# A six-stage layer stack on one core: head pairs' running sums on separate rows, second tile turned first, reordered seams

## What is computed

```python
x = layer_norm(ALPHA * x + ffn, ln_ffn_g, ln_ffn_b)        # end of stages 1 and 3
# stage 4, scan
a_cs = cumsum(dt * A)                                       # per head, over 256 tokens
m = (C @ B.T) * exp(a_cs[l] - a_cs[s])  (s <= l)            # 16 heads
y = m @ (x * dt) + d_skip * x
y = rms_norm((y * silu(z)).reshape(.., 4 groups, 256))      # squares summed by group
# stages 4 and 5, attention group of 8 heads
q, k = rope(rms_norm(q)), rope(rms_norm(k))
o = softmax(mask(q @ k.T / 8)) @ v
```

## Time and profile before

| | us |
|---|---|
| median of 3 runs | 1745.08 (1743.03 to 1753.56) |
| profiled execution, its own time | 1750.59 |
| its span, first to last instruction | 1748.8 |
| TensorE busy | 1618.3 (93%) |
| VectorE, ScalarE, GpSimd busy | 369.8, 269.0, 85.1 |
| mean granted clock of TensorE | 0.988 |

### The profile page before, as it was taken

How to read it: one execution, slowest core, us unless ns; L and a number is a source line. 1 busy time by engine, 2 the same in 40 slices (tenths; PEclk the granted TensorE clock), 3 DMA queues, 4 the chain that set the end, 5 groups by cost and what they waited for, 6 DMA issues and landing times.

```text
span 1748.8 us, 24093 instructions
## 1 busy us (share of the span) xinstructions
PE 1618.3 (93%) x10356; PEld 993.2 (57%) x10356; DVE 369.8 (21%) x796; ACT 269.0 (15%) x647; POOL 85.1 (5%) x148
## 2 busy tenths in 40 slices
PE   8998999988988899989999899888999999999988
PEld 7855555555554576465555555545884444645553
DVE  0933000000000212430000000003324442330322
ACT  2011000000000012210000000001232323311330
POOL 0000000000000000000000000000001233003110
PEclk9999999999999899999999999999999999999998
DMA  9557999999999832579999999998442223244100
GB/s 399 217 217 316 426 428 428 428 426 430 427 427 427 367 144 97 217 315 426 427 428 428 428 428 428 428 427 375 145 145 96 96 97 108 85 144 144 49 0 24
DMA packets 37632, 502.55 MB, mean 287 GB/s; under 512 B 4160, under 2 KB 4288, under 8 KB 5440
## 3 DMA queue, kind: packets, MB, share of 16 engines
q1 hardware_dynamic: 36992, 499.53, 69.3%
q0 software_dynamic: 576, 2.10, 0.3%
HBM read 500.56 MB, written 1.05 MB: 287 GB/s over the span
## 4 chain that ended last, share of the span: by engine, by line
PE 75%; DMA 18%; DVE 3%; issue 2%; ACT 1%; SPq 0%; ACTq 0%; DVEq 0%
DMA ring<-in_expert_up 14%; PE ps L1116 12%; PE ps L614 10%; PE ps L737 9%; PE ps L754 8%; PE ps L802 6%; PE ps L651 6%; PE ps L720 3%; DMA ring<-in_expert_down 3%; PE ps L820 3%; PE ps L1111 2%; PE ps L966 2%; PE ps L942 2%; PE ps L1170 1%; PE ps L591 1%
## 5 line engine op out<-in xcount | busy, mean ns | idle before, releaser
L737 PE MATMUL ps<-x_tok,constants_sb 128*128 128x256 f32 x1184 | 296.8, 394 | 0.0
L754 PE MATMUL ps<-ring,arena 128*32 128x256 f32 x3968 | 240.2, 384 | 44.4 <-DMA ring<-in_expert_up 37.9
L737 PEld LDWEIGHTS ps<-x_tok,constants_sb 128*128 128x128 f32 x1184 | 213.8, 191 | 103.0 <-issue 80.4
L1116 PE MATMUL ps<-ring,spare 128*128 128x512 f32 x480 | 215.5, 603 | 1.8 <-DVE spare L1799 1.7
L754 PEld LDWEIGHTS ps<-ring,arena 128*32 128x32 f32 x3968 | 120.7, 110 | 153.1 <-DMA ring<-in_expert_up 32.0
L614 PE MATMUL ps<-spare,ring 128*128 128x256 f32 x832 | 183.0, 383 | 4.0 <-DVE spare L1799 1.7
L614 PEld LDWEIGHTS ps<-spare,ring 128*128 128x128 f32 x832 | 159.4, 192 | 26.4 <-DVE spare L1796 2.9
L1116 PEld LDWEIGHTS ps<-ring,spare 128*128 128x128 f32 x480 | 89.5, 191 | 111.1 <-issue 108.5
L802 PE MATMUL ps<-ring,arena 128*32 128x512 f32 x960 | 123.2, 613 | 16.0 <-ACT arena L1462 12.0
L2002 DVE TENSOR_TENSOR arena<-arena,ps 128x128 f32<-128x128 f32 x64 | 18.4, 288 | 507.3 <-ACT arena L1467 507.3
L651 PE MATMUL ps<-ring,arena 128*128 128x512 f32 x224 | 101.3, 610 | 1.9 <-DVE arena L2430 1.4
(11 more groups left out here) (279 smaller groups left out, 1291.5 us busy)
## 6 DMA issues: line engine op xcount, KB each, us to landing
ring<-in_expert_up SPq DMA_DIRECT2D x124, 2048.0 KB, 22.7
ring<-in_expert_down SPq DMA_DIRECT2D x46, 2048.0 KB, 26.6
ring<-in_stream SPq DMA_DIRECT2D x44, 2048.0 KB, 8.6
ring<-in_expert_down SPq DMA_DIRECT2D x28, 1024.0 KB, 24.8
arena<-in_expert_up SPq DMA_DIRECT2D x4, 2048.0 KB, 8.2
arena<-in_expert_down SPq DMA_DIRECT2D x2, 2048.0 KB, 10.6
spare<-in_expert_down SPq DMA_DIRECT2D x2, 2048.0 KB, 7.6
constants_sb<-in_constants SPq DMA_DIRECT2D x1, 1574.0 KB, 17.2
```

Source lines behind the costliest of these rows:

```text
L737: pe.matmul(ps[:, b, 0:TOK], ident, x[:, 0, 0:TOK], start=True, stop=True, skip_group_check=True)
L754: ins = pe.matmul(ps[q * SLOTS:(q + 1) * SLOTS, 4 + e % 2, 0:TOK] .rearrange("p (g n) -> p g n", g=2), xg[:, 4 * half + k, e * SLOTS:(e + ...
L1116: ins = pe.matmul(bank(b + part), xT[:, k, part * P:(part + 1) * P], w[:, k, :], start=(k == 0), stop=(k == KT - 1))
```

## The change

1. Bias rows of the norm behind an expert stage: right behind the scatter, ahead of the branch (before: behind it). If the branch is taken they are made again.
2. Warm-ups: in the last quad five instead of four behind each up chunk, four instead of two between down projections; none instead of five at the head of stage 2; nine instead of thirteen at the head of stage 4.
3. The 16 running sums are also put on partitions 64 to 79; `run_sum` of an odd head reads them there.
4. In the scan's last round y(7) and the last projection half stand ahead of the last two square sums.
5. Attention: in the first group of a stage the wait for the last projection's take-up moves behind the first scores, and the wait for `ss_var` behind the first tile's transposes. In the other groups the second tile is turned first, and the wait stands between the tiles; `move_T` on ScalarE and VectorE follows that order.

```diff
@@ -583,7 +583,7 @@
 
-                for b in range(2 * tiles[0], 2 * tiles[-1] + 2):
+                for b in [2 * t + kk for t in tiles for kk in range(2)]:
                     t, kk = b // 2, b % 2
@@ -761,7 +761,7 @@
                             if not (closing and j == 2 * QUAD - 1):
-                                spin(6)
+                                spin(6, SPINS + 1 if closing else SPINS)
                             if opening and j == 0:
@@ -807,10 +807,10 @@
                             pe.wait_ge(s("back_moved"), i + (n2 + 1))
-                            closing()
+                            closing(0)
                         elif closing and k < 3:
                             pe.wait_ge(sem("ln_gain_moved"), rnd + 1)
-                            spin(4, SPINS // 2)
+                            spin(4)
                         elif k < 3 and not closing:
@@ -821,6 +821,8 @@
                         ins.then_inc(s("scattered"), 1)
+                    if closing:
+                        closing(1)
 
@@ -905,7 +907,7 @@
                           lambda j: slot4[slot(b0 + QUAD_CHUNKS + j)],
-                          lambda: norm_rows(0).then_inc(sem("ln_rows"), 1))
+                          lambda which: norm_rows(which).then_inc(sem("ln_rows"), 1))
                 pe.wait_ge(sem("m_counted"), layer + 1)
@@ -920,13 +922,10 @@
                                       None, lambda j: slot4[j % RING])
-                    pe.sem_inc(sem(f"m{layer}_more_over"), 1)
-                norm_rows(1).then_inc(sem("ln_rows"), 1)
+                    norm_rows(1).then_inc(sem(f"m{layer}_more_over"), 1)
 
...
                 g = base[STICK]
-                if MOE0 in on:
-                    keep_warm(5)
                 transposes("x2", x, normed(STICK), (0,))
@@ -1131,12 +1130,19 @@
 
-            def attention(grp, ahead, extra=None):
+            def attention(grp, ahead, extra=None, opening=False):
+                taken_up = projected[0]
+                def ready(t, kk):
+                    if opening and SSD in on and grp == 0 and (t, kk) == (1, 0):
+                        pe.wait_ge(sem("ss_var"), 1)
+                    elif not opening and (t, kk) == (0, 0):
+                        pe.wait_ge(sem("at_proj"), taken_up)
 
                 pe.wait_ge(sem("at_qk"), 2 * (grp + 1))
-                pe.wait_ge(sem("at_proj"), projected[0])
-                transposes(qk_turn(grp), at_qk)
+                transposes(qk_turn(grp), at_qk, ready, (0, 1) if opening else (1, 0))
                 wait_T(qk_turn(grp))
@@ -1196,6 +1202,8 @@
                         mix(pr - 1)
+                    elif opening:
+                        pe.wait_ge(sem("at_proj"), taken_up)
                     turn_p(pr)
@@ -1207,7 +1215,7 @@
                 if MOE1 in on:
-                    keep_warm(13)
+                    keep_warm(9)
                 transposes("h4", at_h, ready, (0,))
@@ -1229,10 +1237,13 @@
                 sums = con[:, CONST["upto"][0]:CONST["ones"][1]]
-                pe.matmul(ps[0:16, 1, 64:64 + TOK], av[:, 0, :], sums, start=True, stop=False,
-                          skip_group_check=True)
-                pe.matmul(ps[0:16, 1, 64 + P:64 + TOK], av[:, 1, :], C("upto"), start=False,
-                          stop=True, skip_group_check=True).then_inc(sem("ss_cs"), 1)
+                for p0 in (0, 64):
+                    pe.matmul(ps[p0:p0 + 16, 1, 64:64 + TOK], av[:, 0, :], sums, start=True,
+                              stop=False, skip_group_check=True)
+                for p0 in (0, 64):
+                    ins = pe.matmul(ps[p0:p0 + 16, 1, 64 + P:64 + TOK], av[:, 1, :], C("upto"),
+                                    start=False, stop=True, skip_group_check=True)
+                ins.then_inc(sem("ss_cs"), 1)
 
@@ -1262,7 +1273,7 @@
                               start=True, stop=True).then_inc(sem("ss_bc"), 1)
-                pe.wait_ge(sem("ss_csT"), 1)
+                pe.wait_ge(sem("ss_csT"), 2)
                 pe.wait_ge(sem("ss_z"), 2)
@@ -1271,8 +1282,11 @@
                         pe.wait_ge(sem("ss_cb"), h + 1)
-                    pe.matmul(ps[:, 4 + h % 2, 0:TOK], ident[0:16, h:h + 1].broadcast_to([16, P]),
-                              ss_csT[0:16, :], start=True, stop=True).then_inc(sem("ss_sum"), 1)
+                    p0 = 64 * (h % 2)
+                    pe.matmul(ps[:, 4 + h % 2, 0:TOK],
+                              ident[p0:p0 + 16, p0 + h:p0 + h + 1].broadcast_to([16, P]),
+                              ss_csT[p0:p0 + 16, :], start=True, stop=True)\
+                        .then_inc(sem("ss_sum"), 1)
 
@@ -1306,15 +1320,15 @@
                         half(*units.pop(0))
-                    if n >= 2:
+                    if 2 <= n < SSD_HEADS // 2:
                         square_sums(n - 2)
...
                         half(*units.pop(0))
+                square_sums(SSD_HEADS // 2 - 2)
                 square_sums(SSD_HEADS // 2 - 1)
-                pe.wait_ge(sem("ss_var"), 1)
-                attention(0, [(kind, g + 9 + n) for n, kind in enumerate("qkv")])
+                attention(0, [(kind, g + 9 + n) for n, kind in enumerate("qkv")], opening=True)
                 attention(1, [(kind, g + 12 + n) for n, kind in enumerate("qkv")])
@@ -1349,7 +1363,8 @@
                 no = 1 if SSD in on else 0
-                attention(g_no(3), [(kind, g + 4 + n) for n, kind in enumerate("qkv")])
+                attention(g_no(3), [(kind, g + 4 + n) for n, kind in enumerate("qkv")],
+                          opening=True)
 
@@ -1389,10 +1404,10 @@
 
-            def move_T(name, dst, scale=1.0, banks=None):
-                for b in banks or ((0, 2) if name[0] == "q" else (0, 1)):
-                    act.wait_ge(transposed, 4 * turn[name] + b + 1)
+            def move_T(name, dst, scale=1.0, banks=None, order=range(4)):
+                for b in banks or (0, 1):
+                    act.wait_ge(transposed, 4 * turn[name] + order.index(b) + 1)
                     kk = b % 2
@@ -1599,7 +1614,10 @@
             def attention(grp, out_g, ahead, between=lambda pr: None):
-                move_T(qk_turn(grp), at_qkT, 0.125)
+                if grp in (0, g_no(3)):
+                    move_T(qk_turn(grp), at_qkT, 0.125, (0, 2))
+                else:
+                    move_T(qk_turn(grp), at_qkT, 0.125, (2, 0), (2, 3, 0, 1))
 
@@ -1783,13 +1801,11 @@
 
-            def move_T(name, dst, banks=None, column=None):
-                if banks is None:
-                    banks = (1, 3) if name[0] == "q" else (2, 3)
+            def move_T(name, dst, banks=(2, 3), column=None, order=range(4)):
...
                     kk = b % 2
-                    dve.wait_ge(transposed, 4 * turn[name] + b + 1)
+                    dve.wait_ge(transposed, 4 * turn[name] + order.index(b) + 1)
                     o = dst[:, 4 * kk:4 * kk + 4, (b // 2) * P:(b // 2 + 1) * P]
@@ -2090,6 +2106,7 @@
                                 .then_inc(sem(f"m{layer}_more_lowered"), 1)
+                    dve.wait_ge(sem(f"m{layer}_more_over"), 1)
                 if stage == MOE1 and SSD in on:
@@ -2180,7 +2197,10 @@
                           last=lambda: None):
-                move_T(qk_turn(grp), at_qkT)
+                if grp in (0, g_no(3)):
+                    move_T(qk_turn(grp), at_qkT, (1, 3))
+                else:
+                    move_T(qk_turn(grp), at_qkT, (3, 1), order=(2, 3, 0, 1))
 
@@ -2277,8 +2297,9 @@
                     d[7], ps[:, 1, 0:32].rearrange("p (t h) -> p t h", t=2), -1.0, None, mul))
-                dve.tensor_copy(ss_csT[0:16, :], ps[0:16, 1, 64:64 + TOK])\
-                    .then_inc(sem("ss_csT"), 1)
+                for p0 in (0, 64):
+                    dve.tensor_copy(ss_csT[p0:p0 + 16, :], ps[p0:p0 + 16, 1, 64:64 + TOK])\
+                        .then_inc(sem("ss_csT"), 1)
                 hd = [P, 8, 64]
```

## The result

The changed kernel takes **1732.83 us** (median of 4 runs, 1731.70 to 1734.14) and the kernel before, beside it on the same chip, 1745.09 (4 runs, 1743.03 to 1753.56). The ratio is 0.9917 with the interval 0.9896 to 0.9937: faster by 0.8%, less than the 1% from which the forecast speaks of faster. The forecast was 1732. The profiled execution took 1732.98 (span 1730.8), 17.6 less than that of before. That is more than the 13.4 forecast, and the two profiles also differ in where and for how long the clock was low: read in stretches of 1 us, some 42 us of before and 34 us of the changed kernel were at 1.2 GHz. So the places are compared by their own lengths, and even these hold some of the clock, as the experiments show.

The account below looks back on a forecast made before the run. The prediction took TensorE (three quarters of the path) and weight transfers (18%) to bound the kernel. Its terms summed to 13.4 us gained, from the 1745.1 us median to 1732, range 1722 to 1741.

Parts of the forecast that it names:

- A: Whole kernel: 13 us gained as summed, about 0.8%; chance 0.55.
- First seam: Seam into stage 2: bias rows right behind the scatter, five warm-ups gone; gain 3.4 us, bounds 1.5 and 5.0.
- Second seam: Seam into stage 4: VectorE's copies of the transposed tile move up; gain 1.9 us, bounds 1.0 and 2.0.
- rival D: Clock stays low behind a seam: 128 matmuls at half speed take 27.9 us more, 1763 us; chance 0.05.
- rival C: Everything lands high and the low clock near the end shrinks: 1724 to 1726 us; chance 0.22.
- Last quads: Expert layers' last quads: extra warm-ups mostly covered by transfers; 0.5 us lost in all, bounds 0 and 1.8.
- Pairs: Scan: head pairs' running sums overlap on separate rows; gain 3.0 us, bounds 0 and 4.2; extra small pair costs 0.1.
- Rival B: Scan: the running-sum pairs don't overlap; whole gain 10.4 us, time 1735 us; chance 0.15.
- Square sums and first group: Scan's end: wait for ScalarE's square gone, gain 1.7 us; first attention group: variance wait behind transposes, gain 0.9.
- Groups 1, 2 and stage 5's second: Attention openings: second tile's transposes run under the wait for v; 0.9 us each, 2.7 in all.
- Stage 5's first: First attention group of stage 5: TensorE starts 1.2 us earlier, ScalarE's copies don't; scores gain 0.4 us.
- Rival E: Seams are not on the path: experts' transfers absorb the first, 8 us are left, 1737 us; chance 0.03.

Follow-up runs that it names:

- warm_back: The changed kernel with five and thirteen warm-ups again at the heads of stages 2 and 4: 1733.98 us.
- rows_late: The changed kernel with only the bias rows put back behind the load and branches: 1735.92 us.
- pairs_only: The kernel before with only the odd heads' running sums moved to partitions 64 to 79: 1746.3 us.
- attn_only: The kernel before with only the later square sums and the changed attention openings: 1741.97 us.
- pairs_again: The kernel before with only the odd heads' running sums moved to partitions 64 to 79, run once more: 1746.67 us.
- seams_only: The kernel before with bias rows right behind the scatter and fewer warm-ups at the heads of stages 2 and 4, last quads as before: 1740.8 us.
- no_spins: The changed kernel with four and two warm-ups in the last quads, as before the change: 1731.52 us.
- no_pairs: The changed kernel with the running sums of all heads on partitions 0 to 15 again: 1736.85 us.
- the filled versions: The changed kernel with warm-ups around stage 4's transposes and the 16-column products split, run twice, then with four attention warm-ups added: 1729.15, 1731.53, 1729.13 us.

## Why the prediction was right

The likeliest case, A, is what came: 12.3 us gained between the medians, by the steps named. The mechanism of the steps was right in the main. The first seam and the last quads were mis-sized, one exposed wait was overlooked, and the clock's moves stood in no term.

- **First seam** (3.4 forecast): 4.91, nearly the upper bound of 5.0. This term was mis-sized. The two bounds of the step were whether the sequencer runs through load and branches while the rows execute, and I took a value between them. It does run through: TensorE was ready early enough to wait 2.43 us for VectorE, and warm_back puts the rest of the load at 1.34 us. VectorE was the path: the second tile's transposes start 11.33 us behind the scatter, and the forecast's "can't start before 591.2" is 11.3. For the same reason the five warm-ups, 4.64 us in the forecast's working, were worth at most 0.85 us once the rows stood ahead (without them ahead 1.8: 18.54 against rows_late's 16.73). But 4.91 is the gain over one profile with a long low stretch. Four profiles of the old seam give 16.52 to 18.55, eight of the new one 13.42 to 13.78; against pairs_only's 16.52, whose low stretch is as long as the changed kernel's, the gain is 2.9. The other 2.0 are the longer low stretch of before's profile (about 1.6) and its longer stall (3.62 against 3.23).
- **Second seam** (1.9): 1.95. VectorE was the path. But behind it the two stretches at 1.2 GHz took 6.4 us in the profiled execution: from the first L614 to the first scan group behind it 58.93 us before and 65.29 after. This is rival D's mechanism, at its own place and a quarter of its size. Its first stretch goes with the four warm-ups taken out there, as the profiles beside warm_back show; the one at the small products also stands in warm_back and in attn_only (1247 to 1251), which have thirteen. The mean clock is 0.9908 over the 63 runs of before and 0.9909 over the 10 of the changed kernel, so the low clock has moved more than grown. The profiles show one place that gave back, the low clock of ten microseconds from 1705 of the earlier trace rows: from its first transposes to the output projection it was 19.03 us (1704.69 to 1723.72) and is 15.54 (1690.22 to 1705.76). That is rival C's, worth 3.5 in this pair of profiles; in pairs_only, pairs_again, attn_only and seams_only the stretch is 3.4 us long, and it is absent in seven of the nine profiles of the changed kernel and its variants. C and D were given as cases apart from A; both came in part, and offset each other.
- **Last quads** (−0.5): 0.05 gained and 0.18 lost, and no_spins shows no difference: 58.98 and 59.09 us against 58.99 and 59.08. The cover, the wait for the transfer, was larger than I allowed.
- **Pairs** (3.0, and −0.1 for the small ones): 8 × 0.42 is 3.4, less the wait of 0.48 us for k's take-up, 2.9; no_pairs shows 2.97. The factor for the overlap was 0.62 by the earlier trace rows and is 0.60. My answer to whether a faster TensorE exposes another engine was "nothing", and that was wrong by half a microsecond: I looked at y, the rotation and the products, not at the take-up of the projection between. The Trainium skill (TensorE: Matmul & The Clock Gate, Part 3) lets row tiles start about 4 ns apart; by that a pair would take 0.53, an estimate from half of the 1.05. The trace shows 0.63, between that and one behind the other. Rival B's 1.05 did not come.
- **Square sums and first group** (1.7 + 0.9): 2.86 from y(6) to the scores (12.22 to 9.36), the same 2.86 in attn_only.
- **Groups 1, 2 and stage 5's second** (2.7): the first scores move up against their surroundings by 0.93 us each, 2.8. **Stage 5's first** (0.4): 0.41, and the copies behind ScalarE's table load (1.28 us, from 1609.47) hold the rest, now as a wait of 1.76.
- **Sum by lengths**: 4.91 + 1.95 + 2.97 + 2.86 + 2.8 + 0.4, less 0.1 for the last quads, is 15.8. Measured, between medians 12.3, at equal clock 12.7. Of the 3 us between, 2.0 can lie in the first seam: with 2.9 there, the gain at a like low stretch, the sum is 13.8, 1.1 above 12.7 and about the uncertainty. That is argued from one profile, pairs_only's. It fits that rows_late too showed 3.0 of 5.7 at equal clock, with longer low stretches in its seams. Rival E, transfers that absorb the first seam's gain, is not needed for it and not excluded as a part. (Its 8 us are what is left when both seams' 5.3 are absorbed, not the first alone.)

The forecast's total was right with some luck: by their lengths the first seam gained 1.5 us more than forecast and the last quads lost 0.4 less, the sum of lengths is 3 us more than the time shows, and low clock that came at one place went at another.

## What to carry to other kernels

Work whose operands are ready goes ahead of a load and branch on the engine's sequencer: the small matmuls then execute while the branch is decided, and that place was worth more than the filler matmuls taken out. Filler that stands in front of a wait for another engine costs little there; taken out at the second seam it shortened nothing, and the clock fell behind it. Once the bias rows moved, TensorE and VectorE changed roles at the seam, so a second edit there has to be sized against the new wait, not the old. Where a whole kernel's runs spread with the mean granted clock, write that clock beside every time, and judge a 3 us edit by the length of its own place in the trace as well, with the low clock inside both places compared: the same seam, untouched, was 16.52 to 18.55 us long.

## What the hardware showed that I had not expected

- The spread of one kernel's runs, up to 16 us, goes with the mean granted clock: one slope of 1.37 us per 0.001 fits eleven kernels and leaves 1.4 us. A 0.8% change is about 0.009 of it.
- Two matmuls of 16 rows on rows 0 and 64 take 0.63 us together, where on the same rows they take 1.05.
- A load and branches that stood for 3.04 to 3.63 us at the seams leave 1.13 to 1.54 when the bias rows (1.99 us, L901) are queued ahead; only at the first seam without warm-ups is nothing of them seen, under the wait for VectorE.
- The clock fell to 1.2 GHz behind waits of about 1.1 and 1.7 us around the second tile's transposes, and around products of 16 columns, in the profiles of the changed kernel (both times), no_spins, no_pairs and seams_only. rows_late has only the first, warm_back and attn_only only the second, and before, both pairs kernels and the three runs of the filled versions neither.
